# One gate block moved from the end of a recurrence into the last row tiles of an attention, and one square root taken earlier

## The reference, cut to what matters

```python
h = rms_norm(x, norm_mix)
proj = h @ w_in
hq, hf, hi, hog, dq, dk, dv, gate_hg, gate_da = split(proj)   # the gates: 1024 columns each
o_hg = hgrn2_chunked(hq, 1 - f, hi, log(f))                   # 4 heads, 16 chunks of 64 rows
o_hg = rms_norm(o_hg, hg_out_norm) * silu(hog)
y_hg = o_hg @ w_branch_hg
o_da = diff_attention(q1, q2, k1, k2, v, lam)                 # 4 heads, blocks of 128 queries, causal
y_da = rms_norm(o_da, da_out_norm) * (1 - lam_init) @ w_branch_da
mixed = sigmoid(gate_hg) * y_hg + sigmoid(gate_da) * y_da
x = x + mixed @ w_out
# then a mixture of experts, and a second block of another kind
```

## Time and profile before

| what | us |
|---|---|
| median of 3 runs (lowest, highest) | 2735.91 (2733.3, 2736.36) |
| the profiled execution | 2732.7 |
| its span, first to last instruction | 2730.9 |
| TensorE matmul busy | 2641.0 (97%) |
| TensorE weight loads busy | 2204.3 (81%) |
| VectorE busy | 1828.6 (67%) |
| ScalarE busy | 1324.7 (49%) |
| GpSimd busy | 401.6 (15%) |
| mean granted TensorE clock | 0.991 of full speed |

### The profile page before, as it was taken

The page is one execution under the profiler, slowest core; times in us unless marked ns, Lnnn a source line. Parts: engine busy times, 40 slices in busy tenths (PEclk is TensorE's granted clock), DMA queues, the critical chain, the costliest instruction groups (busy, mean ns, idle before and its releaser), DMA issues. The chain is left out here.

```text
span 2730.9 us, 37181 instructions
## 1 busy us (share of the span) xinstructions
PE 2641.0 (97%) x13682; PEld 2204.3 (81%) x13682; DVE 1828.6 (67%) x2466; ACT 1324.7 (49%) x1950; POOL 401.6 (15%) x351
## 2 busy tenths in 40 slices
PE   8999999989999999999999999989999999999999
PEld 7888876878788888888888888778878878888887
DVE  5761475457434788888888767666625885857878
ACT  3112243567422477877787322455533553525353
POOL 0222212100230122222221012300020000000000
PEclk9999999999999899999999999999999999999999
DMA  3115124311452499999999332100031616253441
GB/s 130 51 47 182 40 74 145 113 43 47 156 172 109 175 372 377 390 380 372 373 371 358 139 105 63 43 1 1 1 131 54 266 52 246 73 188 139 155 184 62
DMA packets 141881, 435.74 MB, mean 160 GB/s; under 512 B 23344, under 2 KB 45616, under 8 KB 110000
## 3 DMA queue, kind: packets, MB, share of 16 engines
q1 hardware_dynamic: 124736, 400.30, 40.8%
q0 software_dynamic: 10656, 20.99, 2.2%
q10 hardware_dynamic: 6352, 12.58, 1.2%
HBM read 387.68 MB, written 63.96 MB: 165 GB/s over the span
## 5 line engine op out<-in xcount | busy, mean ns | idle before, releaser
L2552 DVE TENSOR_TENSOR w_lo<-w_raw,w_hi 128x2048 fp32r<-128x2048 f32 x192 | 437.3, 2294 | 65.7 <-ACT w_hi L2486 60.2
L2486 ACT ACTIVATE w_hi<-w_raw 128x2048 fp32r<-128x2048 f32 x187 | 355.9, 1925 | 39.6 <-PE banks L2611 39.6
L3469 PE MATMUL banks<-b_parts,a_parts 128*128 128x512 f32 x1344 | 306.9, 390 | 6.3 <-DVE a_parts L3524 6.3
L3469 PE MATMUL banks<-a_parts,b_parts 128*128 128x512 f32 x1344 | 306.0, 390 | 2.3 <-DVE a_parts L3524 1.2
L3469 PEld LDWEIGHTS banks<-b_parts,a_parts 128*128 128x128 f32 x1344 | 252.0, 188 | 60.7 <-DVE a_parts L3524 8.8
L3469 PEld LDWEIGHTS banks<-a_parts,b_parts 128*128 128x128 f32 x1344 | 252.2, 188 | 55.0 <-DVE a_parts L3524 1.6
L3498 ACT ACTIVATE b_parts<-w_quarter 128x1024 fp32r<-128x1024 f32 x112 | 118.6, 1059 | 280.5 <-PE banks L3469 265.9
L638 POOL TENSOR_TENSOR w_lo<-w_raw,w_hi 128x512 fp32r<-128x512 f32 (+2 forms) x132 | 158.1, 1203 | 587.0 <-ACT w_hi L617 585.8
L617 ACT ACTIVATE w_hi<-w_raw 128x512 fp32r<-128x512 f32 (+2 forms) x132 | 74.1, 574 | 324.2 <-PE banks L696 302.2
L696 PE MATMUL banks<-w_hi,act_hi 128*128 128x512 f32 (+1 forms) x576 | 219.3, 381 | 8.1 <-DVE act_lo L1848 3.4
L3518 DVE TENSOR_TENSOR b_parts<-w_quarter,b_parts 128x1024 fp32r<-128x1024 f32 x112 | 136.9, 1222 | 132.4 <-ACT b_parts L3498 132.4
(11 more groups left out here) (523 smaller groups left out, 5569.1 us busy)
## 6 DMA issues: line engine op xcount, KB each, us to landing
w_raw<-in_w SPq DMA_DIRECT2D x192, 1024.0 KB, 7.4
a_parts<-scratch_x_parts SPq DMA_DIRECT2D x42, 1024.0 KB, 4.8
w_raw<-in_w_in SPq DMA_DIRECT2D x80, 256.0 KB, 2.7
w_quarter<-in_w_up SPq DMA_DIRECT2D x16, 1024.0 KB, 6.9
w_quarter<-in_w_down SPq DMA_DIRECT2D x16, 1024.0 KB, 7.3
scratch_x_parts<-a_parts SPq DMA_DIRECT2D x14, 1024.0 KB, 4.4
scratch_gateT<-gate_staged SPq DMA_DIRECT2D x32, 256.0 KB, 2.1
gate<-scratch_gateT SPq DMA_DIRECT2D x32, 256.0 KB, 3.7
```

Source lines behind the costliest of these rows:

```text
L2486: act.activation(hi[c % SLOTS][:, :], raw[c % TILES][:, :], ACT.Copy).then_inc(hi_done, 1)
L2552: dve.tensor_tensor(lo[c % SLOTS][:, :], raw[c % TILES][:, :], hi[c % SLOTS][:, :].bitcast(F32), ALU.subtract).then_inc(lo_done, 1)
L3469: mm = pe.matmul(out, left, right, start=(start and n == 0), stop=(stop and n == 2))
```

## The change

Block 7 of the gates is no longer made in the recurrence but in the attention: `HG_BLOCKS` goes from 8 to 7. The rest of the fill behind the last head is 26 matmuls instead of 74, and the copies 14 and 15 and the rounding of block 9 leave ACT's list there; on SyncE one load and two stores go. All later halves keep their place in the attention's order, counted by halves: the first one made there is 14 instead of 16. Halves 26 and 27 now have bank 7 alone, as 28 to 31 had. In the attention the fills of the last four row tiles grow from 9, 6, 4, 1 to 11, 9, 7, 5 a unit, 48 in all. The root of the last head is taken between the copies 12 and 13. The ranges of `full_at` and `parts` and the first block of POOL's loop are fitted to the new count; the latter still begins with block 9.

```diff
-GATE_BLOCKS, HG_BLOCKS = 2 * ND, ND
+GATE_BLOCKS, HG_BLOCKS = 2 * ND, ND - 1
@@
             squares(3)
             gates.keep(act, 12)
+            roots(2, HG_H - 1, HG_H)
             gates.keep(act, 13)
             gates.high(act, 8)
-            roots(2, HG_H - 1, HG_H)
-            gates.keep(act, 14)
-            gates.keep(act, 15)
-            gates.high(act, 9)
@@
-    FIRST_FILL, FILL = 16, (20, 20, 18, 14, 9, 6, 4, 1)
+    FIRST_FILL, FILL = 16, (20, 20, 18, 14, 11, 9, 7, 5)
     fills = [(FILL[i] // 2, FILL[i] - FILL[i] // 2) for i, _ in units]
     FIRST = 2 * HG_BLOCKS
     total = np.cumsum([FIRST_FILL] + [x for pair in fills for x in pair]).tolist()
-    full_at = [next(j for j, n in enumerate(total) if n >= BLOCK_MM * (m + 1)) for m in range(FIRST)]
-    parts = {(p, f): [FIRST + m for m in range(FIRST) if full_at[m] == 1 + 2 * p + f] for p in range(n_units) for f in range(2)}
+    full_at = [next(j for j, n in enumerate(total) if n >= BLOCK_MM * (m + 1)) for m in range(2 * GATE_BLOCKS - FIRST)]
+    parts = {(p, f): [FIRST + m for m in range(2 * GATE_BLOCKS - FIRST) if full_at[m] == 1 + 2 * p + f] for p in range(n_units) for f in range(2)}
@@
-            for b in range(HG_BLOCKS + 1, GATE_BLOCKS):
+            for b in range(HG_BLOCKS + 2, GATE_BLOCKS):
                 gates.low(pool, b)
```

## The result

The changed kernel is a little slower. In 12 runs of each the medians were 2738.11 us after (2736.83 to 2742.68) and 2733.14 us before (2731.05 to 2737.86); the ratio is 1.0021, with a 95% interval of 1.0013 to 1.0028, some 5.7 us. The forecast said 5.4. The profiled execution took 2737.48 us with a span of 2735.7, at a mean granted clock of 0.990.

The account below looks back on a forecast made before the run. TensorE, busy 97% of the span, bounds the kernel, but the recurrence's end waits for POOL's stores. Terms -1.5 - 0.4 + 7.4 - 0.1 = +5.4 us on 2735.9 gave 2741.3 us, own range 2739 to 2743.5, overall range 2735 to 2746.

Parts of the forecast that it names:

- The two steps by which the forecast would have called itself wrong: Recurrence and attention: POOL's drain not ending near 467, or units 28 to 30 keeping their 14.0 us.
- The tail: End of the recurrence: drain still follows POOL's four stores, shorter only by the gate stores' bytes; -1.5 us, bounds 0.5 to 2.5.
- The last root: End of the recurrence: root sooner, DVE's chain ends some 6 us sooner, but POOL's stores don't wait for it; 0.
- a DVE held up behind the new subtraction of block 15: Attention, behind unit 18: by the shared-port rule POOL's subtraction could hold DVE by its whole length, 2.39 us.
- The start of attention: Before the first scores: block 9's subtraction no longer runs there, so DVE's lambda product shortens; -0.4 us (0 to 0.5).
- The wider stand: PE before attention: stands some 14 us instead of 4.9; up to 0.7 us lost at low clock, none taken.
- Exposed matmuls and bank waits: Attention units 16 to 31: 32 of 48 added matmuls exposed, +7.4 us; moved waits for bank 7 together -0.1.
- The five new or vanished waits: Attention, by running sum of fills: waits of 19 and 23 go (-3.7); new in 18 (+2.2), 21 (+0.5), 27 (+0.7).
- the tail gives all: Rival, end of the recurrence: drain follows ACT or PE, stage ends 11 us sooner; sum -4.0, 2731.9 us; chance 0.07.
- the late units have room: Rival, late attention units: DVE's or ACT's chain hides more matmuls; sum +1.5, 2737.4 us; chance 0.20.
- more waits than the one priced: Rival, units 18 to 20: rounding and POOL subtraction behind the copy add +2 to +4; with +3, 2744.3 us; chance 0.20.
- nothing was misplaced: Rival, attention fills: a fill or bank not as the sums say, showing in the halves' places; 2736 us; chance 0.03.

Follow-up runs that it names:

- e1: Kernel before with only the last root taken sooner, behind the copy of half 12; ratio to the kernel before 0.9996 (0.9987 to 1.0005).
- e2: Changed kernel with POOL's four stores of o_hg ahead of its subtraction for block 8; ratio to the kernel before 0.9989 (0.9980 to 0.9997).
- e3: Changed kernel with fills of before and block 15 of the gates left out, its 48 matmuls made nowhere; ratio to the kernel before 0.9996 (0.9987 to 1.0005).
- e4: Kernel before with fills 8, 6, 4, 2 instead of 9, 6, 4, 1, so gate halves end with a unit; ratio 0.9980 (0.9971 to 0.9989).
- e6: Changed kernel with stores of o_hg first and fills 8, 12, 6, 6 instead of 11, 9, 7, 5; ratio to the kernel before 0.9971 (0.9960 to 0.9982).
- e5: Kernel before with the last root sooner and POOL's stores of o_hg ahead of its subtraction for block 8; ratio 0.9992 (0.9983 to 1.0001).
- e9: Kernel before with root sooner, stores first, fills 8, 6, 4, 2 and lambda and output-gain loads issued in the recurrence; 2723.27 us, ratio 0.9958.
- e8: Changed kernel with stores first, fills 8, 12, 6, 6 and lambda and output-gain loads issued in the recurrence; 2724.1 us, ratio to the kernel before 0.9966.
- e7: Kernel before with root sooner, stores of o_hg first and fills 8, 6, 4, 2; ratio to the kernel before 0.9974 (0.9965 to 0.9983).

## Why the prediction was right

The working of the forecast is compared term by term, on the two profiled executions. From the copy of half 12 to the branch stage's first load it is 243.18 - 236.36 = +6.8 us, where the forecast had +5.4; the medians say +5.0, the ratio 1.0021 +5.7 with 3.6 to 7.7 inside its interval. The two steps by which the forecast would have called itself wrong, where the drain ends and what units 28 to 30 cost, both held. Three terms were mis-sized, by 0.6, 0.5 and 0.4 us, all to the same side. That the whole kernel's difference is nearer to 5.4 than this sum is luck: in the profiled executions 1.7 us came back behind the branch stage's first load, where nothing was changed, and 0.3 had come before half 12.

- **The tail, -1.5 forecast, -0.9 measured** (19.93 and 19.91 us against 20.81, 20.82 and 20.86). The mechanism is the forecast's: the stage ends by POOL's drain behind four stores, at 467.7 where "near 467" was said. The size wasn't. The stores' packets took the DMA engines 7.4 us in the changed kernel (61.8% of 12) and 7.3 before. From their first issue to the end of the drain it was 10.3 us instead of 11.1, so of the 1.5 us that the gate stores' packets took, 0.8 delayed the drain. The rest must have run in gaps of the stores' own packets, which is worked out here and not seen by itself. The forecast named that case as its bound (0.5) and took the whole.
- **The last root, 0 forecast, 0 measured** (e1). That DVE's product took 2.13 us only because of POOL's subtraction is shown too: moved away from it, it took 0.17. The Trainium skill, SBUF — State Buffer, section "SBUF: two separate sides", has both engines on one port with an exclusive lock; the two numbers agree with that rule. What the forecast feared by it, a DVE held up behind the new subtraction of block 15, didn't come: unit 19 shrank by its 1.67, and no further load waits there. Nor was it put to the test: the subtraction (592.17 to 594.57) met only two of DVE's maxima over scores in the banks (0.82 us each).
- **The start of attention, -0.4 forecast, +0.1 measured.** DVE's product did shrink (0.73 to 0.29), but began 4.63 us after the first load instead of 4.11, because the loads it waits for landed later in this execution. In e2 and e3, with the same instructions, the start was 7.80 and 7.83, 0.35 less than before, so the term is right in sign and size and the changed kernel's profiled execution, outside the term's bounds of 0 to -0.5, didn't have it. The wider stand, 14.9 us, cost nothing: the clock was low at the restart after 4.9 us already.
- **Exposed matmuls and bank waits, 7.4 - 0.1 = +7.3 forecast, +7.7 measured.** By the forecast's terms, unit by unit from 16 to 31 (the length of a unit, from its first scores to the next one's), forecast against measured: 0.70/0.70, 0/0.22, 2.16/1.93, -1.66/-1.67, 0.70/0.69, 0.52/1.05, 0.47/0.01, -0.92/-0.91, 0.70/0.69, 0/0.47, 0.47/0.01, 1.38/1.37, three times 0.93/0.97, 0/0.19. The five new or vanished waits were all where the running sum put them. Two small misses: in unit 21 ACT's copy cost 1.2 us as a wait before a gate matmul, while the `aT` wait behind it fell from 1.88 to 1.12, which is the three matmuls hidden there (0.70) and only 0.06 more; and the matmuls counted as exposed in 22 and 26 were hidden, as one of unit 17's and two of unit 25's weren't, so that a pair of neighbours has the right sum and the wrong places: in 17 and 18 together 2.15 against 2.16, in 21 and 22 1.06 against 0.99, in 25 and 26 0.48 against 0.47.
- **The rivals.** That the tail gives all is ruled out by e3. That the late units have room is too: the twelve of 28 to 30 cost 2.9 us. The copy with a rounding in unit 18 made no more waits than the one priced, and the waits lie in the units that the running sum gives, so nothing was misplaced.

The forecast didn't ask whether its waits could be had for nothing, and there the larger sums lay. All the waits before a gate matmul that it moved about, -3.7 and +3.4, can be taken away by fills with the same sum (e4: -5.0, e6: -4.4), and the 11 us that PE had been relieved of in the tail are 7.7 if POOL's list is turned round (e2).

That leaves the price of the change itself, with everything else in order: it takes 7.7 us from the tail (e5 to e2) and costs 217.21 - 209.02 = 8.2 us in the attention (e9 to e8), 8.7 without e9's fall of the clock at 624. The 48 matmuls are 11.0 us of PE (48 x 0.23), of which some 3 us are hidden in the one place and 2 to 3 in the other.

What stays open is where the 1.7 us behind the branch stage's first load came from. It lies within what executions differ by: with the same instructions in all eleven kernels but for e3's gate reads, the stretch from that load to the end of the span took 2046.2 us before, 2044.5 after, and 2043.0 to 2048.3 in all of them. And the median of the runs shown before (2735.9) lay 1 to 3 us above the medians of before that were measured beside the other kernels, so that the time forecast (2741.3, with a range of its own from 2739) was 3.2 above that measured, with a difference that was 0.3 off.

## What to carry to other kernels

Before work is taken from an engine at a stage's end, read what the stage's exit waits for: here it was a queue's drain behind its stores, and the relieved engine only stood longer until the stores were issued ahead of other work in that queue. Where filling work is drawn by a running count, put its buffer boundaries at the places at which the buffer's reader is idle anyway; that was worth 4.4 to 5 us here, with the same number of matmuls. And the same 48 matmuls cost about as much in the one stage as in the other (7.7 and 8.2 to 8.7 us), as both were bound by the same engine once the waits were gone: look for waits before looking for another place.

## What the runs showed of the hardware

**The clock falls behind short stands too, and not always.** In e1, e5 and e7 PE stood 2.5, 3.9 and 3.85 us before the first scores, at full clock until then; the granted clock was at 0.50 for a little over three microseconds soon after, and it cost 1.6 to 1.7 us. Behind 2.0 us there in e2 and 1.76 in e9 it stayed at 1.00. It fell again in e1 just after 600, behind unit 19's wait of 2.17 (1.6 us), and in e1, e3, e5 and e9 behind unit 25's wait of 2.4 for `aT` (0.5 to 0.6 us each); behind the same two waits the kernel before kept 1.00, and behind the second also e4 and e7. Windows of before and of e3:

```profile
630.00:640.00 10.00, 7.13 (x48) 5.66 (x47) 6.57 (x11) 6.80 (x15) 0.00 (x0) 1.00 0.01 2
630.00:640.00 10.00, 8.54 (x49) 7.67 (x50) 6.57 (x10) 6.79 (x15) 0.00 (x0) 0.83 0.01 2
```

That the stand causes the fall isn't shown, only that it lay ahead each time. The Trainium skill, TensorE: Matmul & The Clock Gate, section "Why this matters for your kernels", warns of idle gaps between bursts of matmuls. The stands of 3.9 us agree with it; those of 2.2 to 2.5 are shorter than the gaps it names, and there the measurement decides.

**A block's exit on POOL includes the data of its stores.** In the changed kernel the drain ended 6.8 us after the last store's issue was over (460.93 to 467.7) and 0.7 after the stores' last packet. In e2, with the stores ahead of the subtraction, their last packet ended at 457.1, the subtraction at 458.14 and the drain at 458.9, 0.75 behind the later of the two.

**A short VectorE product beside a GpSimd subtraction** took 2.13 us instead of 0.17 and 0.73 instead of 0.29; in e4 it was 0.90.
